# Expert gates of a mixture layer: 16 matrix products of 64 columns in place of 32 of 32 columns, with the halves added on VectorE

## The reference, cut to what matters

```
# xt: 256 tokens x 1024; every token picks 8 heads x 16 experts and a gate for each
experts = e1 * 128 + e2                      # per token 128 picked experts
gates   = softmax(sv)                        # per token 128 gates
hid     = gelu(sum_d xt[t, d] * u_tab[experts[t, k], d])
out     = sum_k gates[t, k] * hid[t, k] * v_tab[experts[t, k]]
```

## Time and profile before

| | us |
|---|---|
| median of 3 runs | 3125.11 |
| lowest and highest run | 3121.54, 3132.65 |
| the profiled execution | 3134.55 |
| its span, first to last instruction | 3132.7 |
| TensorE busy | 3058.0 |
| VectorE busy | 2271.7 |
| ScalarE busy | 1376.4 |

### The profile page before, as it was taken

The page is one execution under the profiler, slowest core; times in us unless marked ns, Lnnn a source line. Parts: engine busy times, 40 slices in busy tenths (PEclk is TensorE's granted clock), DMA queues, the critical chain, the costliest instruction groups (busy, mean ns, idle before and its releaser), DMA issues. The chain is left out here.

```text
span 3132.7 us, 59178 instructions
## 1 busy us (share of the span) xinstructions
PE 3058.0 (98%) x22446; PEld 2675.2 (85%) x22446; DVE 2271.7 (73%) x3842; ACT 1376.4 (44%) x2167; POOL 248.3 (8%) x195
## 2 busy tenths in 40 slices
PE   8899999999999989999999999999999999999999
PEld 7699988989888869998998988776678877886999
DVE  7678877787887868887777798775547674576446
ACT  5445344443444544534344344444532223446444
POOL 0064000000000007200000000100001010001000
PEclk9999999999999999999999999999999999999999
DMA  4245555474555324546556456420026552232354
GB/s 166 84 139 195 169 200 203 157 247 157 164 181 208 128 75 155 201 163 226 178 181 224 158 168 207 162 88 21 1 74 209 188 197 85 86 109 88 128 182 155
DMA packets 131891, 478.44 MB, mean 153 GB/s; under 512 B 14592, under 2 KB 16640, under 8 KB 131328
## 3 DMA queue, kind: packets, MB, share of 16 engines
q1 hardware_dynamic: 115904, 416.72, 39.8%
q0 software_dynamic: 15808, 59.25, 5.8%
HBM read 474.87 MB, written 1.05 MB: 152 GB/s over the span
## 5 line engine op out<-in xcount | busy, mean ns | idle before, releaser
L1698 DVE TENSOR_TENSOR Wl<-ring,Wh 128x1024 fp32r<-128x1024 f32 x720 | 878.7, 1222 | 559.1 <-ACT Wh L1207 556.9
L545 PE MATMUL bank<-HR,Wh 128*128 128x256 f32 (+1 forms) x7488 | 1142.9, 303 | 6.6 <-DVE HR L1918 4.0
L1207 ACT CAST Wh<-ring 128x1024 fp32r<-128x1024 f32 x788 | 824.4, 1047 | 609.4 <-PE bank L545 608.7
L545 PEld LDWEIGHTS bank<-HR,Wh 128*128 128x128 f32 x7488 | 1011.9, 191 | 65.4 <-issue 13.8
L545 PE MATMUL bank<-HR,Wl 128*128 128x256 f32 (+1 forms) x3744 | 610.1, 299 | 10.1 <-DVE Wl L1698 10.1
L545 PE MATMUL bank<-Wh,HR 128*128 128x512 f32 x2304 | 577.1, 393 | 1.1 <-DVE HR L2105 0.8
L545 PEld LDWEIGHTS bank<-HR,Wl 128*128 128x128 f32 x3744 | 523.5, 191 | 34.0 <-DVE Wl L1698 11.6
L545 PEld LDWEIGHTS bank<-Wh,HR 128*128 128x128 f32 x2304 | 428.4, 188 | 96.2 <-issue 8.4
L545 PE MATMUL bank<-arena 128*128 128x32 f16 (+5 forms) x5128 | 310.3, 214 | 15.4 <-DVE arena L1877 6.2
L545 PE MATMUL bank<-Wl,HR 128*128 128x512 f32 x1152 | 306.0, 389 | 0.0
L1436 ACT ACTIVATE arena<-bank 128x256 f32 (+1 forms) x256 | 98.5, 385 | 470.3 <-PE bank L545 470.1
(11 more groups left out here) (254 smaller groups left out, 2164.6 us busy)
## 6 DMA issues: line engine op xcount, KB each, us to landing
ring<-weights SPq DMA_DIRECT2D x788, 512.0 KB, 3.4
HA<-mods POOLq DMA_DIRECT2D x48, 512.0 KB, 4.1
arena<-mods POOLq DMA_DIRECT2D x48, 512.0 KB, 3.6
arena<-bias POOLq DMA_DIRECT2D x16, 256.0 KB, 3.2
arena<-keys POOLq DMA_DIRECT2D x2, 1024.0 KB, 5.3
arena<-mla POOLq DMA_DIRECT2D x1, 1536.0 KB, 6.6
X<-x SPq DMA_DIRECT2D x1, 1024.0 KB, 6.6
X<-context POOLq DMA_DIRECT2D x1, 1024.0 KB, 7.2
```

Source lines behind the costliest of these rows:

```text
L545: return nc.tensor.matmul(out, lhsT, rhs, start=first, stop=last)
L1207: nc.scalar.copy(Wh[:, i % SPL], ring[:, i % RAW]).then_inc(S("hi_done"), 1)
L1698: v.tensor_tensor(Wl[:, i % SPL], ring[:, i % RAW], Wh[:, i % SPL], ALU.subtract).then_inc(S("lo_done"), 1)
```

## The change

In u1, u2 and u3 (the phases of kind u) a step becomes 16 products of 64 columns: for each token the high and the low 32 columns side by side, each token's weights loaded once. Eight tokens fill a bank, so a step fills banks 2 and 3 both. ScalarE copies the low columns of both banks into `gate_lo`, VectorE adds the high columns to them into `gate_sum`, waits for that and multiplies the hidden values by `gate_sum`. Both buffers lie in the room of `Hh` and `Hl` that the phases of kind u leave unused. TensorE starts gate n when the sums of step n-1 are done. VectorE's order at a gate in these phases becomes `spread` n+2, then `gated` n. ScalarE's list of u1 is written out instead of looped. In v2 the steps stay as they were, except that every fourth one waits for the product of the step before, not of the one before that.

```diff
+        gate_lo, gate_sum = HA4[:, 0, 2:4, 0:T], HA4[:, 1, 2:4, 0:T]
+        def gate_parts(b, part):
+            return bank[2 + b][:, :].rearrange("p (t d e) -> p d t e", d=2, e=EQ)[:, part]
...
-                    def gate(s, it=0, qb=qb):
+                    def gate(s, it=0, qb=qb, kind=kind):
...
-                        after(pe, S("gm_ev"), n - 1)
+                        if kind == "u":
+                            after(pe, S("gs_ev"), N_SIDE * l + qb * GS + s + R // 2 * it)
+                            for i in range(BT):
+                                at = 2 * EQ * (i % (BT // 2))
+                                m = mm(bank[2 + i // (BT // 2)][:, at:at + 2 * EQ].rearrange("p (d e) -> p d e", d=2),
+                                       Aoh[s % 2][:, i // 2, :, i % 2], Bg[s % 2][:, :, i // 2, :, i % 2], True, True)
+                            m.then_inc(S("g_mm"), 1)
+                            return
+                        after(pe, S("gm_ev"), n - 1 if s else n)
...
+                    def gate_low(it, s, qb=qb):
+                        n = qb * GS + s + R // 2 * it
+                        act.wait_ge(S("g_mm"), N_GATE * l + n + 1)
+                        after(act, S("gs_ev"), N_SIDE * l + n)
+                        for b in range(2):
+                            m = nc.scalar.copy(gate_lo[:, b, :].rearrange("p (t e) -> p t e", e=EQ), gate_parts(b, 1))
+                        m.then_inc(S("gl_ev"), 1)
...
+                            if pi == 1 and R * it + s >= GATELESS:
+                                i = GATED_AT[R * it + s - GATELESS]
+                                if GATED_U1[i - 1:i] == ["g"]:
+                                    gate_low(0, GATED_U1[:i].count("g") - 1)
+                            elif pi > 1 and s % 2 == 0:
+                                gate_low(it, s // 2)
                             following_high(it, s)
...
-                    steps(act, EQ // R, False, body, True)
+                    if pi == 1:
+                        for it in range(EQ // R):
+                            body(it)
+                    else:
+                        steps(act, EQ // R, False, body, True)
...
                     g = GH[qb % 2][:, :, at]
+                    if qb < NQ - 1:
+                        i = N_SIDE * l + qb * GS + s + R // 2 * it
+                        dve.wait_ge(S("gl_ev"), i + 1)
+                        after(dve, S("gm_ev"), n)
+                        for b in range(2):
+                            m = v.tensor_tensor(gate_sum[:, b, :].rearrange("p (t e) -> p t e", e=EQ), gate_parts(b, 0),
+                                                gate_lo[:, b, :].rearrange("p (t e) -> p t e", e=EQ), ALU.add)
+                        m.then_inc(S("gs_ev"), 1)
+                        dve.wait_ge(S("gs_ev"), i + 1)
+                        g = g.rearrange("p e (b t) -> p e b t", b=2)
+                        v.tensor_tensor(g, g, gate_sum.rearrange("p b (t e) -> p e b t", e=EQ), ALU.mult).then_inc(S("gm_ev"), 1)
+                        return
...
                             if what == "g":
-                                gated(0, n, qb)
                                 if n + 2 < GS:
                                     spread(0, n + 2, qb)
+                                gated(0, n, qb)
...
+                                if kind == "u" and (s + 4 < R or not last(it)):
+                                    spread(it, s // 2 + 2, qb)
                                 gated(it, s // 2, qb)
-                                if s + 4 < R or not last(it):
+                                if kind == "v" and (s + 4 < R or not last(it)):
                                     spread(it, s // 2 + 2, qb)
```

More of the change, by code:

```diff
@@ L31 @@
 N_GATE = NQ * GS
+N_SIDE = (NQ - 1) * GS
 R = 8
@@ L53 @@
 GATED_U1 = (["g", "t", "t"] * 3 + ["g", "t"]) * 4
+GATED_AT = [i for i, what in enumerate(GATED_U1) if what == "t"]
 GATES_TURN = 0
```

## The result

Before: median 3125.32 us of 18 runs. After: 3133.09 of 18 runs (3127.86 to 3136.19). The ratio is 1.0024, 95% interval 1.0017 to 1.0031: 7.8 us slower, inside the 0.3% that the prediction calls no change, but above its range, and on the other side of its 3111.

What follows compares the result with a forecast made beforehand. TensorE, busy 98%, was taken as the bound. u2 and u3 -22.0 us, u1 +5.9 and ends of u3 +1.8 made -14.3, from the median 3125.11 to 3111; range 3099 to 3127.

Steps and rivals of the forecast that it cites:

- Part 1: TensorE's gate step: 16 products of 64 columns at 29.1 ns take 0.54 us, saving 0.34; u2's period becomes 6.30.
- Rivals B: Gate products on TensorE cost 40 ns a pair, as with 32-bit weights; total 3126 us; chance 0.10.
- D: Gate products on TensorE cost their columns, 50.6 ns, so only the waits remain; total 3140 us; chance 0.07.
- The rule of the Trainium skill: TensorE's load and product both count, about 81 ns a pair at 128 columns; estimated 54 ns at 64, no gain.
- Part 2: VectorE's list in u2 grows from 5.27 to 6.17 us, product unchanged at 0.59; fits 6.30, costing nothing in u2 and u3.
- rival C: VectorE's list in u2 and u3 reaches 6.67 us, with 0.25 more on each sum; total 3142; chance 0.08.
- point of decision of 6.5: VectorE list of about 6.5 us, at which the gain of u2 and u3 (-9) equals the losses elsewhere.
- the slack: In u2, VectorE's list of 6.17 us against the period of 6.30 leaves 0.13 to spare.
- Part 3: Single pair of banks: no wait in u2; three u1 stalls of 2.5 us; u1 2.9 longer, u3's end 0.9, per layer.
- rival E: One-tile stalls of u1 do not appear, as sums come earlier; 15 us less, 3096; chance 0.05.
- The sentence on the granted clock: TensorE's granted clock might fall after the stalls of u1, which no row let the prediction price.
- Part 4: ScalarE's two copies of some 0.38 us each, u1's unrolled list, v2's stricter wait and the later ring loads cost nothing.

Runs made afterwards that it cites:

- e1_layout: The changed kernel with low halves and sums stored tokens innermost, so the product reads them in one run; 3115.66 us, 0.9970 of before.
- e3_both: The changed kernel with sums stored tokens innermost and `gated` put ahead of `spread` again; 3097.44 us, 0.9912 of before.
- run 693: Not a follow-up run's label: in e1_layout the product, reading its operand from SBUF in one unbroken run, is 693 ns long.
- e4_clock: The changed kernel with eight idle 16-bit products of 512 columns in each stall of u1, into an unread bank; 3128.34 us, 1.0014 of before.
- e2_order: The changed kernel with `gated` put ahead of `spread` again, layout left as changed; 3115.76 us, 0.9967 of before.
- e5_pair: The changed kernel with two pairs of banks in turn in u1, so a gate waits for sums of two steps before; 3120.65 us, 0.9985 of before.

## Why the prediction was wrong

**Part 1 held.** A pair of 64 columns was forecast at 29.1 ns and costs 0.49/16 = 30.6; the period without waits is 6.32 (e1_layout, e3_both) for a forecast 6.30. Rivals B (40 ns) and D (50.6) fall. The rule of the Trainium skill that the prediction weighed ("TensorE: Matmul & The Clock Gate", section "Back-to-back issue gap"), from which an estimate of 54 ns came, is not borne out by these rows either.

**Part 2 failed, at "The product is unchanged at 0.59, its rows reading PSUM".** The sums came as forecast (565.18 - 564.29 = 0.89, forecast 0.90); the product, which I gave neither bounds nor a rival, takes 1.05 to the next start instead of 0.59. The row that I used reads the same step of 128 bytes, but from PSUM. The list is 6.58, not 6.17. What the runs showed in place of the 0.59: from SBUF in steps of 128 bytes the product is 1128 ns long, in one run 693 (e1_layout). The list of 6.58 is rival C's mechanism and beyond its point of decision of 6.5, with the excess on the product instead of the sums; C's own 3142 was not reached, since u2 and u3 still won a little. With the product at 0.61 (e3_both) the list fits, and nothing waits inside u2 and u3: the slack was real. e1_layout is the prediction with this one term mended: u2 and u3 win 5.3 and 4.5 a layer (forecast 5.5 and 4.6), u1 loses 4.7 (forecast 2.9, and 1.5 of the rest is one fall of the clock), and its 3115.66 lies inside the range of 3099 to 3127. In after, u2 won 2.6 a layer instead of 5.5, u3 0.9 instead of 4.6, since the end of u3 met the lag as a wait of 1.66 in place of the 0.9 forecast.

**Part 3 held in its mechanism, and missed the clock.** Stalls of 2.78, 2.29 and 2.30 stand before the gates that the prediction names, so rival E falls; the intervals are 6.37, 5.89 and 5.90 for a forecast 5.90. But u1 lost 7.2 a layer, not 2.9. Of the 4.3 between, 3.0 are the two intervals of 7.82 and 7.80 behind the stalls; e4_clock, which takes the lower clock out of u1, gives these 3.0 back. Of the rest, VectorE's list in u1 (6.36, from the spread at 331.05 to the next at 337.41, for a forecast 5.96) makes the first stall longer by 0.47, the second and third interval 6.38 and 6.35, and the wait at the end 0.98 where e1_layout has 0.64. The first interval of 6.55 has another cause, for e1_layout has it too and e2_order and e5_pair have 6.32 or 6.33: it needs the sums behind the spread and the single pair. The sentence on the granted clock named the clock as what no row could price, but the sum put it at nothing and the range did not carry it.

**Part 4 held.** ScalarE's copies of 0.38 are on no path: in after VectorE's sums never wait for them, and no wait of v2's gates for the step before appears in after.

**The account.** Forecast were -14.3 us, measured in the stretches +7.4. The 21.7 between are 8.6 in u1, 5.7 in u2 and 7.4 in u3. Mending the layout alone gives 17.4 back, mending the order alone 17.3, both 35.7 (medians against 3133.09). That the first two add up to nearly the third is luck, for the stretches of layer 0 do not add: layout, order and both give 2.6, 6.5 and 11.0 in u1 (more together), 2.6, 2.3 and 2.6 in u2 (either one does it, or nearly) and 3.6, 0.2 and 3.6 in u3 (the layout alone). The sums in place of the product from PSUM were a good trade; where they were stored and where VectorE took them cost more than it won.

**Open.** Why the granted clock fell after some of the stalls and not after others of the same length (2.25 in e1_layout, 2.29 and 2.30 in after, 1.66 to 1.79 at the start of v2 in after and e4_clock) was not settled. No run has two pairs of banks in u2 and u3, so how far a second pair would have made up for the long list there is not shown.

## What to carry to other kernels

Price an operand by the memory it lies in and by the step at which it is read, not by its size alone; when an edit moves it, the old row no longer prices it, and the layout belongs among the bounds. When a buffer becomes single, put its consumer first in the consumer's list; what stands ahead of it becomes part of the producer's wait (u1's first stall is 0.81 in e2_order and 2.78 in after). A list longer than the period binds only when the room ahead of the wait is used up, so count the lag over the phase, and look for it at the phase's end.

## What the runs showed of the hardware that I had not expected

VectorE's product reads its 32-bit operand from SBUF in steps of 16, 64 or 128 bytes 1.7 to 1.8 times slower per element, by the estimate above, than in steps of 8 or in a run. From PSUM, steps of 128 bytes (0.68 us for 512 elements, 693 ns for one run from SBUF) and of 256 bytes (e1_layout's sums, 416 ns, as in after, where they read runs) cost nothing. ScalarE's copy of 256 elements from PSUM, 379 ns when it writes one run to SBUF, takes 644 and 658 when it writes in steps of 64 and 16 bytes. After waits of TensorE of 1.69 to 2.78 us the granted clock was in some cases 0.52 to 0.67 over the next three microseconds, with a tile of 4.18 us in place of 2.95, and in others, after waits of 1.66 to 2.30, 1.00.
